# A gated HGRN2 and gMLP block on eight cores: the last stage in three token passes, and residual squares summed in fp32

## What is computed

```
h = rmsnorm(x, norm_mix);  proj = h @ w_in           # q, f, inp, g, u, v, two gates
y_a = HGRN2 scan over the sequence (8 heads of 128), normed, gated, @ w_a_out
y_b = (gelu(u) * spatial(layernorm(gelu(v)))) @ w_b_out
x = x + (sigmoid(gate_a) * y_a + sigmoid(gate_b) * y_b) @ w_o
x = x + square(relu(rmsnorm(x, norm_ffn) @ w_ff1)) @ w_ff2
x = x + sigmoid(rmsnorm(x, norm_ple) @ w_ple_gate) * (p @ w_ple_proj)
return rmsnorm(x, norm_final)
```

## Time and profile before

| | us |
|---|---|
| time, median of 3 (2005.83 to 2272.36) | 2006.55 |
| the profiled execution's own time | 2006.55 |
| its span on the slowest core (core 2) | 2004.6 |
| spans of the other cores | 1996.2 to 2002.0 |
| PE busy in the span | 1945.9 (97%) |
| DVE busy | 653.7 (33%) |
| ACT busy | 581.2 (29%) |

### The profile page before, as it was taken

One profiled execution on the slowest core, in us unless ns is written; L12 is line 12 of the kernel. 1 busy time (PEld: TensorE's weight loads), 2 busy tenths in 40 slices (PEclk: granted clock), 3 DMA queues, 4 the chain that ended last, 5 costly groups with the idle time before them and its releaser, 6 DMA issues.

```text
span 2004.6 us, 24277 instructions; the slowest of 8 cores (1996.2 to 2004.6 us)
## 1 busy us (share of the span) xinstructions
PE 1945.9 (97%) x9202; PEld 898.7 (45%) x9388; DVE 653.7 (33%) x1044; ACT 581.2 (29%) x816; POOL 115.2 (6%) x236
## 2 busy tenths in 40 slices
PE   6999999999999999999999999999999999999995
PEld 2444455444444444444444444444444444444442
DVE  4745535453722112222112121212122112222576
ACT  4574417365111111123432003300231013333442
POOL 0000011111100000000000000000000000000000
PEclk9999999999999999999999999999999999999998
DMA  9872443344474545454444344344343466443313
GB/s 212 192 166 44 85 85 64 71 88 118 117 150 90 121 85 113 98 113 77 75 73 84 68 79 84 66 83 77 71 85 70 78 104 119 82 76 72 64 48 121
DMA packets 28753, 188.67 MB, mean 94 GB/s; under 512 B 3168, under 2 KB 3424, under 8 KB 8160
## 3 DMA queue, kind: packets, MB, share of 16 engines
q0 software_dynamic: 22016, 152.84, 41.6%
q1 hardware_dynamic: 6624, 34.27, 5.2%
HBM read 331.54 MB, written 8.39 MB: 170 GB/s over the span
## 4 chain that ended last, share of the span: by engine, by line
PE 92%; DMA 3%; DVE 2%; issue 1%; ACT 1%; POOL 0%; SPq 0%; DVEq 0%; POOLq 0%; ACTq 0%
PE ps L484 92%; DMA W_52<-wb 2%; DMA XF_77<-xT 1%; DVE XT L467 0%; ACT L445 0%; PE ps L494 0%; ACT RSTD L445 0%; DVE VTG L474 0%; SPq L498 0%; DVE TMPS_140 L943 0%; POOL ST_142 L462 0%; DVE ST_141 L961 0%; DVE UU L462 0%; POOL ST_141 L462 0%; DVE ST_142 L961 0%
## 5 line engine op out<-in xcount | busy, mean ns | idle before, releaser
L484 PE MATMUL ps<-HT,W_51 128*128 128x512 bf16 x1251 | 282.3, 379 | 3.6 <-DVE HP L474 1.8
L484 PE MATMUL ps<-HT,W_53 128*128 128x512 bf16 x1253 | 283.2, 379 | 1.4
L462 DVE TENSOR_TENSOR XT<-XT,ps 128x512 f32<-128x512 f32 x160 | 110.1, 688 | 395.5 <-PE ps L484 392.4
L445 ACT ACTIVATE ps<-ps 128x512 f32<-128x512 f32 x144 | 83.8, 582 | 512.6 <-PE ps L484 512.5
L462 DVE TENSOR_TENSOR ps<-ps,RSTD 128x512 f32<-128x512 f32 x144 | 99.9, 699 | 369.8 <-ACT ps L445 355.7
L484 PEld LDWEIGHTS ps<-HT,W_51 128*128 128x128 bf16 x1280 | 124.6, 98 | 151.4 <-issue 2.6
L484 PEld LDWEIGHTS ps<-HT,W_53 128*128 128x128 bf16 x1280 | 125.1, 98 | 149.4
L484 PE MATMUL ps<-HT,W_52 128*128 128x512 bf16 x751 | 169.5, 382 | 3.2 <-DMA W_52<-wb 2.4
L484 PE MATMUL ps<-HT,W_54 128*128 128x512 bf16 x752 | 168.3, 379 | 1.2 <-ACT ZGR_95 L445 0.4
L445 ACT ACT_TABLE_LOAD x77 | 98.8, 1283 | 88.9 <-PE ps L484 78.2
L484 PEld LDWEIGHTS ps<-HT,W_52 128*128 128x128 bf16 x768 | 75.3, 98 | 92.7 <-issue 5.2
(11 more groups left out here) (447 smaller groups left out, 2108.5 us busy)
## 6 DMA issues: line engine op xcount, KB each, us to landing
W_54<-wb POOLq DMA_DIRECT2D x35, 1024.0 KB, 8.2
W_51<-wb POOLq DMA_DIRECT2D x34, 1024.0 KB, 8.3
W_52<-wb POOLq DMA_DIRECT2D x34, 1024.0 KB, 8.1
W_53<-wb POOLq DMA_DIRECT2D x34, 1024.0 KB, 8.3
XF_77<-xT SPq DMA_DIRECT2D x8, 512.0 KB, 17.8
XF_78<-xT SPq DMA_DIRECT2D x8, 512.0 KB, 9.0
XS_132<-xpT SPq DMA_DIRECT2D x4, 1024.0 KB, 9.6
XS_133<-xpT SPq DMA_DIRECT2D x4, 1024.0 KB, 14.0
```

Of the source, the lines that this page charges most:

```text
L445: return P.op("act", lambda e: e.activation(out=out.ap, in_=in_.ap, func=func, **kw), rd, [out], c, tab=TABLES.get(func, 0))
L462: return dve(lambda e: e.tensor_tensor(out=out.ap, in0=a.ap, in1=b.ap, op=op), [a, b], [out], fsz(a.ap), eng=eng)
L484: fns.append(lambda e, o_=o_, l_=l_, r_=r_, st=st, sp=sp: e.matmul(o_.ap, l_.ap, r_.ap, start=st, stop=sp))
```

## The change

- In the two projections `sq_inline` and its deferral go. `acc_sq` squares each column block on ACT (the first straight into an fp32 buffer ACC, one per half, the others into bf16) and adds it to ACC on DVE. `acc_sum` rounds ACC to bf16 (hi), takes the difference (lo), also bf16, and two matmuls by ones sum both.
- The last stage runs in three passes over tokens: 512, 288 and 224. The first pass uses `acc_sq`, the other two a matmul by ones per column block, put behind the next block's groups (`late`). The embedding matmuls stand ahead of the dense group. `scale_out` of a pass runs within the next, that of the third after the end; outputs go in groups of 4, 4 and 2 columns.
- In the input phase `sq_pair` adds in place, in ACT's buffer. The second and third weight block wait for pieces 5 and 7 of half 0. The first loads of the other half's x wait for the fourth weight block.

```
         if add:
-            s2 = nsq()
-            tt(s2, a_, b_, ALU.add)
-            pr = [(PS[6 + hf], ONESB, s2, c == 0, c == 14)]
+            tt(a_, a_, b_, ALU.add)
+            pr = [(PS[6 + hf], ONESB, a_, c == 0, c == 14)]
...
-    wq.append(w_issue(after=[x0[4]], pieces=2))
-    wq.append(w_issue(after=[x0[6]], pieces=2))
+    wq.append(w_issue(after=[x0[5]], pieces=2))
+    wq.append(w_issue(after=[x0[7]], pieces=2))
     x1 = load_half(1, after=[wfirst["n"]])
     wq.append(w_issue(after=[x1[4]]))
+    w3n = wlast["n"]
...
             if hf == 0 and g < 2:
-                n.raw.add(x1[6].i)
+                n.raw.add(w3n.i)
...
+    def acc_sq(acc, x, first):
+        if first:
+            act(acc, x, AF.Square)
+            return
+        sq = nsq().s(0, fsz(x.ap))
+        act(sq, x, AF.Square)
+        tt(acc, acc, sq, ALU.add)
+    def acc_sum(acc, bank, more=False):
+        n = fsz(acc.ap)
+        hi, lo = nsq().s(0, n), nsq().s(0, n)
+        dve(lambda e: e.tensor_copy(out=hi.ap, in_=acc.ap), [acc], [hi], n, rate=0.5)
+        tt(lo, acc, hi, ALU.subtract)
+        mms(None, [(bank, ONESB, hi, True, False), (bank, ONESB, lo, False, not more)], [ONESB, hi, lo], [bank])
...
                     if stats:
-                        sq_inline(n, hf)
+                        acc_sq(ACC[hf], xt(n, hf), n == 0)
...
+    PASS = [(0, 512), (512, 288), (800, 224)]
...
+    for p, (t0, nt) in enumerate(PASS):
+        last = p > 0
...
+            dense(b2, [WPP.s(c * 2048 + n * 128, c * 2048 + n * 128 + 128) for c in range(2)],
+                  [tok_(PTB, c) for c in range(2)])
+            dense(b, [w.s(c * 256 + jj * 128, c * 256 + jj * 128 + 128) for c in range(16)],
+                  [tok_(HT, c) for c in range(16)])
+            if late:
+                late.pop(0)()
...
+            if last:
+                sq = nsq().s(0, nt)
+                act(sq, x, AF.Square)
+                late.append(lambda sq=sq, n=n: mms(None, [(bank, ONESB, sq, n == 0, n == 15)], [ONESB, sq], [bank]))
+            else:
+                acc_sq(acc, x, n == 0)
+            if p:
+                scale_out(n, p - 1)
```

## The result

The changed kernel takes 1996.47 us (median of its runs) where the kernel before takes 2006.2: a ratio of 0.995, with a 95% interval of 0.9927 to 0.9972. The forecast was 1995.4 us within 1988 to 2003. The span of the slowest core is 1995.1 us (core 6; the others 1987.1 to 1994.2).

A forecast was written before the change was run, and what follows sets the result against it. PE's streamed columns were taken to bound the kernel from 540 to 1983 us, but not the first 160 and last 22 us. From 2006.55, -4.3 + 2.1 + 0.5 - 7.0 - 2.5 = -11.2 gave 1995.4 us, range 1988 to 2003.

The forecast's parts named there:

- Projections: Two projections: 20 fewer matmuls by ones on PE, the added DVE and ACT work and longer root chain hidden; -4.3 us.
- Narrow matmuls: Last stage on PE: matmuls of 288 and 224 columns at interpolated 0.1224 and 0.0957 us, plus matmuls by ones; +2.1 us.
- third rival: Last stage: narrow matmuls pay for their weight loads, making the kernel slower than before, 2009.9 to 2051.9 us; chance 0.03.
- Stalls at the pass boundaries: Last stage: ACT's table loads hold up sigmoids while PE's banks cover three blocks; +0.5 us, bounds 0 and 2.
- first rival: Narrow passes of the last stage: DVE becomes the bound, adding 9.9 us for 2005.3, mostly between 1998 and 2003; chance 0.14.
- Tail: Last dense group to end: shorter chain, scalings and landing, 14.6 against 21.7 us; -7.0 us, including 0.3 for DVE lag.
- the late transfer of the second pass's last columns: Tail: 590 KB output waits for the third pass's last addition, lands in 3.3 to 5 us, in time for 10 us.
- Input phase: First 160 us: three edits to PE's order, waits for loads and buffer release; -2.5 us, from 2 lost to 6.9 gained.
- The weight blocks: Input phase: second block asked for one piece of x later, no shift taken, bounds 0 and +2; order gains 0.4 twice.
- The other half's x: Input phase: its first loads wait for the fourth weight block, on SP's queue, with only later loads of the same kind behind.
- The in-place sums: Input phase: they hold ACT's two buffers until PE has read them, 2.6 us per pair; no wait, narrowly.
- second rival: Input phase gives nothing or loses 2 us, so the kernel takes 1998 to 2000 us; chance 0.13.

The follow-up runs named there:

- The kernels with 160 and 128: Changed kernel with passes of 512, 352, 160 tokens (second and third weight block also asked for as before): 1994.5 us; with passes of 512, 384, 128: 2000.5 us.
- The two-pass kernel: Changed kernel with the last stage in two passes of 512 tokens instead of 512, 288 and 224: 2005.3 us, ratio 0.9988.

## Why the prediction was right, and where it was not

- **Projections: right, -4.6 for -4.3.** The forecast counted whole projections; by the marks it is 23 matmuls by ones less (27 old, 4 new), 5.0 us, and two embedding matmuls more, 0.4. PE ran without a gap, and the kernel with this part alone is 4.7 us under the one before. The 20 matmuls of the forecast and the 23 of this stretch differ by three that stand behind the mark. The longer chain to the root is hidden, as was said.
- **Narrow matmuls: right, +2.3 for +2.1.** Interpolated prices between 128 and 512 columns held to 0.0001 us. The 0.2 is the marks: three matmuls by ones of the projections fall into this stretch (0.65), two embedding matmuls fall out of it (0.43). The third rival (weights that don't hide) is refuted at 288, 224 and 128 columns.
- **Stalls at the pass boundaries: +0.5 forecast, none measured.** The cover of three banks is enough at 288 and 224. The kernels with 160 and 128 (last stage 130.2 and 133.1 us) show that the mechanism is real and where it starts.
- **DVE as the bound (first rival): not at 224, yes at 128.** The forecast allowed DVE 1.69 us per block by adding durations; from start to start it takes less (a block's work ends 0.24 to 0.41 us before the next one can begin at 1.82).
- **Tail: right in its working, -7.8 for -7.0.** Core 2, from which it was worked out, had one of the shorter tails of before; in the mean over the cores the tail falls from 22.4 to 13.7, by 8.7, which is beyond the bound of -8.1. The lag of 0.3 allowed for DVE did not come, and the chain was 0.3 shorter still. The output of 896-byte rows kept up, and the late transfer of the second pass's last columns was in time. The two-pass kernel ties the gain to the third pass.
- **Input phase: the step that failed, +0.5 for -2.5** in the slowest cores of the two profiles, and -0.3 by the times with and without all three edits. Its parts:
  - *The weight blocks.* "The block itself is asked for one piece of x later; the queues are full there, so its data land when the same bytes have moved, and I take no shift (bounds 0 and +2)" is wrong, and the reason with it. The request is what keeps the queues full: put behind one more piece, it leaves them at 0.71 to 0.75 from 24 to 30 us instead of 0.96 to 1.00, and the block is used 1.4 to 2.0 us later. The order that goes with it was to gain 0.4 twice. Instead half 1 starts 18.6 us after the block in the mean of the five profiles as changed and 18.2 in the three as before, PE waits twice for its first sums, and the clock falls in 24 of 40 cores. Block and order together cost 1.2 to 1.8 us, near the upper bound. How much is the block and how much the order is not settled, since no kernel has one without the other.
  - *The other half's x.* The wait for a second-cycle block did go. It is there in 9 of the 24 cores with the input phase as before and in none of the 88 others; but these all have two of the three edits or more, so that putting the other half's x later removed it, as the forecast has it, is not shown. The step "behind it stand only later loads of the same kind" looked at the queue and left out the planner, whose new order makes PE wait 1.3 us near 140 us. The prediction had named a new wait ahead of 160 us as a sign of being wrong.
  - *The in-place sums*, "no wait, narrowly", gain some 1.4 us (1996.6 against 1998.0). 0.8 of it are two waits of PE that are 0.4 us shorter, one near 90 us and one in the middle stretch; the rest is not settled. It is no chance of one profile: over all executions the mean span of the cores is 1993.5 us without them and 1992.4 with them.
- **The second rival** (the input phase gives nothing or loses, 1998 to 2000) was right on the phase and wrong on the time: the tail's extra 0.8, the absent stalls of 0.5 and 0.4 us less around the span (2.0 before, 1.5 now) put the profiled execution at 1996.6. The forecast of 1995.4 came so close partly by luck: 3.0 us too much from the input phase stand against these three.

## What to carry to other kernels

A last stage that ends in a chain over all tokens is shortened by cutting its tokens unevenly: the tail goes with the width of the last pass, and the limit is somewhat above the width at which the engine that evicts needs longer per block than PE, since it has also to work off what piled up at the pass boundary. Compute it from start-to-start times and not from durations: 1.26 against 1.57 us at 192 columns, 1.19 against 1.31 at 160, where the gain was gone, 1.12 against 1.06 at 128. When a load is put behind another one, ask what is left for the queues to move in between, who waits for the load that now comes later, and what order the planner makes of it. And where the cores of a chip differ by luck of their loads, the slowest core counts, and one profile of eight cores doesn't settle a microsecond; the spans of all cores in all executions settle more.

## What the runs showed of the hardware

- Matmuls of 128 to 512 columns with weights of their own run at 0.0556 (128), 0.0956 (224), 0.1225 (288) and 0.2156 us (512) from start to start at full granted clock, in runs of hundreds: the weight loads of 98 ns lie wholly beside them, even where a load is longer than the matmul it feeds.
- DVE's operations overlap: an addition of 128 columns that is shown with 0.28 us starts 0.20 us behind the one before, one of 224 with 0.38 starts 0.30 behind, and 16 scalings of 224, of 0.447 each by the view of groups, take 5.89 us, 0.37 each.
- The granted clock of PE fell to 0.51 (the level of 1.2 GHz) for some 4 us after PE had waited 2.20 and 0.70 us with one matmul between, and 10 matmuls of 512 columns ran there in the time of 20. It happened in some cores and not in others that run the same list: 24 of 40.
- The spread of the cores over the first 200 us (some 8 us) is kept to the end: all later stretches of a core are equal within 0.1 us up to the last dense group.
